# High and low parts of the values in one stationary operand, with the halves of the result added by GpSimd

## The chip, the cores and the metric

The kernel runs on one NeuronCore of a Trainium2 chip. The metric is the time of one execution on the device, in microseconds, as the median of several runs. TensorE does the matrix products and transposes and writes them to PSUM, VectorE and ScalarE read PSUM and SBUF, GpSimd works on SBUF, and the SyncE queue issues nearly all the transfers. The engines run each their own list of instructions in order and wait for each other on semaphores.

## The reference

One layer of a decoder on 1024 tokens of width 1024, in float32: sliding-window attention (16 query heads, 4 key/value heads of width 64, blocks of 128 queries that see their own block and the one before), a squared-ReLU MLP and a gated embedding. The part that matters here is the attention:

```python
q = rmsnorm(q, gq)
k = rmsnorm(k, gk)
kb, vb = band(k), band(v)          # the block before and the block itself: 256 keys
scores = einsum('bnqkgd,bnskd->bnkgqs', qb, kb) * HD ** -0.5
scores = scores - slopes[:, :, None, None] * dist
scores = where(mask, scores, -inf)
m = maximum(scores.max(axis=-1), sink)
e = exp(scores - m[..., None])
probs = e / (e.sum(axis=-1) + exp(sink - m))[..., None]
o = einsum('bnkgqs,bnskd->bnqkgd', probs, vb)
return o.reshape(b, s, H * HD) @ wo
```

## The kernel before

TensorE takes float32 data in a reduced form (`F32R`), so every operand is kept as two parts: a high part, rounded by a ScalarE copy, and a low part, which VectorE makes as the original minus the high part. A product is then three products, high·high, high·low and low·high (`PASSES`).

The attention stage goes over 8 blocks of 128 queries (`n`), and in each over 4 groups (`j`), one for each key/value head with its 4 query heads. Blocks 1 to 5 are one hardware loop, blocks 0, 6 and 7 are written out. The order is written by hand and is the same on all engines; in each group's turn work of several steps is interleaved:

- TensorE (`body`, L1808): the scores of group j, part of the projection of the next block (`project`; "q0" are query heads 0 to 7, "q8" heads 8 to 15, "k" keys and values), transposes of q or k, the product with the values of group j-2 (`weigh_values`), and the transposes of the probabilities of group j-1 (`turn_probs`).
- VectorE (`body`, L1326): bias and row maxima (L1298), the negated maximum (L1303), the reciprocal, the scaling of the probabilities as four instructions (L1316), the low parts of pT (L1323), and in group 1 the low part of the values (L1282), in group 3 that of kT (L1264).
- ScalarE (`body`, L919): the exponentials (L895), the copy of the result of group j-2 from PSUM to RES (`attention_out`, L913), the high parts of pT (L905), in group 1 the high part of the values (L868).
- GpSimd (`body`, L707): variance and power -0.5 for the norms (`head_norm`, `row_norm`), the sink column of the probabilities (`place_sinks`), and the move of keys and values from the slot "this block" to the slot "block before" (`shift_k`, `shift_v`, L680).

The values are kept in `vz`, with zeros between the heads. A stationary operand is 128 columns wide and holds the 64 values of one head beside 64 zeros; taken 64 columns further left, it holds the zeros first. So two products of 256 columns put the even heads of a group into the upper 64 partitions of one PSUM tile of 128x256 and the odd heads into the lower 64. With two slots of keys, three passes and two halves these are 12 matmuls for a group (L1799). One ScalarE copy takes the 128x256 result to RES and counts the semaphore `attended`. TensorE waits for it before the next product, since there is one PSUM bank for it (`pv_bank`).

In block 7 there is no next block to project. There the weights `wo` of the output projection are split instead: ScalarE makes high parts (`wo_hi_unit`, L821), VectorE (L1374) and GpSimd (L696) four low parts each, and TensorE begins with `project_out` (L1859). At the program's start GpSimd clears `vz` and `kT` (L651, L652) and makes the bias tables (L668), and the first block's key norm stands behind ten of these.

After the attention stage come the output projection, the MLP (L1936, L1976, L1997, L2017) and the gate (L2040, L2053), nearly all of it on TensorE without a gap.

## Time and profile before

| | us |
|---|---|
| median of 3 runs | 1142.11 (1141.85 to 1143.12) |
| profiled execution, its time | 1143.35 |
| profiled execution, span from first to last instruction | 1141.6 |
| attention stage, up to the last product with the values | 0 to 308 |
| one block in the loop | 32.8 |
| busy: TensorE / VectorE / ScalarE / GpSimd | 1107.6 / 765.5 / 453.7 / 252.9 |

Times of a trace are counted from the start of the span. A row of an engine gives the start, the duration, the line in the kernel, the tiles written and read, and in brackets how long the engine had been idle and for whom. Matmuls are pipelined: a single row is longer than the time from one to the next, and the chain of waits gives the latter.

### The profile page before, as it was taken

The page shows a single profiled execution, that of the slowest core. Times are in us where ns is not written, and L with a number is a line of the kernel's source. Part 1 is how long each engine was busy: PE and PEld are TensorE (multiplying, and loading weights), DVE is VectorE, ACT ScalarE, POOL GpSimd, SP SyncE. Part 2 cuts the span into 40 slices and gives each one's busy share as a digit, 9 for nine tenths or more (in the row PEclk, how much of TensorE's full clock was granted, in tenths as well). Part 3 has the DMA queues.
Part 4 walks back from the last instruction along what each step waited for, and adds up shares of the span by engine and source line. Part 5 has one row for each costly group of instructions (what it writes and reads, how often), then busy time and mean ns, then how long its engine had stood idle before and what let it go on. Part 6 is the DMA issues. An engine that isn't in the chain of part 4 may idle for free.

```text
span 1141.6 us, 15063 instructions
## 1 busy us (share of the span) xinstructions
PE 1107.6 (97%) x5418; PEld 930.1 (81%) x5418; DVE 765.5 (67%) x1129; ACT 453.7 (40%) x796; POOL 252.9 (22%) x230
## 2 busy tenths in 40 slices
PE   7899999998999996999999999999999999999998
PEld 6788888886888885888888888888888888888887
DVE  5788887888553588766766676668777774564321
ACT  5565666566432314233223323553333332243100
POOL 6532322323100185324532450000000000010000
PEclk9999999999999998999999999999999999999999
DMA  7000000013142404332533234899888882111211
GB/s 277 20 19 20 18 18 18 18 34 151 38 153 87 148 19 166 148 145 114 203 148 144 115 133 144 340 408 345 286 293 289 291 287 77 38 37 56 84 40 44
DMA packets 61801, 154.41 MB, mean 135 GB/s; under 512 B 5040, under 2 KB 6064, under 8 KB 61744
## 3 DMA queue, kind: packets, MB, share of 16 engines
q1 hardware_dynamic: 61600, 153.12, 37.4%
q8 instruction: 36, 0.59, 0.2%
q10 hardware_dynamic: 144, 0.52, 0.1%
q14 instruction: 21, 0.17, 0.0%
HBM read 119.55 MB, written 34.08 MB: 135 GB/s over the span
## 4 chain that ended last, share of the span: by engine, by line
PE 80%; DVE 10%; POOL 3%; ACT 3%; issue 3%; DMA 0%; ACTq 0%; DVEq 0%; POOLq 0%
PE pair L1997 23%; PE pair L1976 23%; PE pair L2040 8%; PE pair L1859 6%; PE pair L1731 5%; PE pair L2017 4%; ACT probs L895 2%; PE pair L1799 2%; PE pair L2053 2%; PE pair L1770 2%; DVE probs L1298 2%; DVE probs L1316 1%; PE pair L1936 1%; PE pair L1906 1%; PE pair L1782 1%
## 5 line engine op out<-in xcount | busy, mean ns | idle before, releaser
L1997 PE MATMUL pair<-uT 128*128 128x512 f32 x1176 | 266.7, 389 | 0.0
L1997 PEld LDWEIGHTS pair<-uT 128*128 128x128 f32 x1176 | 220.7, 188 | 45.8
L1126 ACT ACTIVATE uT<-wo_raw 128x1024 fp32r<-128x1024 f32 x63 | 63.9, 1053 | 105.0 <-PE pair L1997 89.4
L638 POOL TENSOR_SCALAR row_var<-row_ssq 128x1 f32<-128x1 f32 x24 | 4.6, 192 | 437.0 <-ACT hn L1023 430.3
L1572 DVE TENSOR_TENSOR uT<-wo_raw,uT 128x1024 fp32r<-128x1024 f32 x63 | 74.8, 1221 | 39.5 <-ACT uT L1126 39.5
L1731 PE MATMUL pair<-WA,xT 128*128 128x512 f32 x384 | 96.4, 401 | 1.4 <-DVE kn L1255 1.0
L1859 PE MATMUL pair<-WA,oT 128*128 128x512 f32 x384 | 91.6, 396 | 2.3 <-DVE WA L1374 1.7
L1859 PEld LDWEIGHTS pair<-WA,oT 128*128 128x128 f32 x384 | 72.4, 191 | 17.6 <-issue 1.9
L1731 PEld LDWEIGHTS pair<-WA,xT 128*128 128x128 f32 x384 | 70.7, 191 | 17.4 <-issue 2.9
L895 ACT ACTIVATE probs<-probs,nmax 128x257 f32<-128x257 f32 x128 | 63.7, 500 | 52.3 <-DVE nmax L1303 52.1
L1976 PE MATMUL pair<-WA,WB 128*128 128x512 f32 x312 | 74.4, 396 | 3.6 <-ACT xr L1101 3.6
L1976 PEld LDWEIGHTS pair<-WA,WB 128*128 128x128 f32 x312 | 59.6, 191 | 16.6 <-issue 4.0
L1976 PE MATMUL pair<-uT,WB 128*128 128x512 f32 x264 | 61.6, 389 | 0.0
L1976 PEld LDWEIGHTS pair<-uT,WB 128*128 128x128 f32 x264 | 49.5, 188 | 10.3
L1799 PE MATMUL pair<-pT,vz 128*128 128x256 f32 x384 | 52.5, 286 | 0.7 <-DVE pT L1323 0.7
L1799 PEld LDWEIGHTS pair<-pT,vz 128*128 128x128 f32 x384 | 48.9, 190 | 3.4 <-DVE pT L1323 2.2
L775 POOL TENSOR_TENSOR hn<-RES 128x1024 f32<-128x1024 f32 x7 | 22.3, 3187 | 120.4 <-DVE RES L1558 120.4
L1679 DVE TENSOR_TENSOR act_buf<-pair,act_buf 128x512 f32<-128x512 f32 x16 | 11.0, 690 | 55.3 <-PE pair L2053 55.3
L1298 DVE CUSTOM_DVE_ANT_0 probs<-pair,bias 128x256 f32<-128x256 f32 x128 | 46.3, 418 | 0.2 <-PE pair L1770 0.2
L1731 PE MATMUL pair<-WB,xT 128*128 128x512 f32 x192 | 45.3, 392 | 0.7 <-DVE xT L1230 0.7
L1638 DVE TENSOR_TENSOR RES<-RES,pair 128x512 f32<-128x512 f32 x48 | 30.8, 681 | 22.2 <-PE pair L1997 22.2
L2017 PE MATMUL pair<-WA 128*128 128x512 f32 x192 | 45.4, 393 | 0.0
(182 smaller groups left out, 2074.7 us busy)
## 6 DMA issues: line engine op xcount, KB each, us to landing
wo_raw<-in_m_w SPq DMA_DIRECT2D x53, 512.0 KB, 6.5
wo_raw<-hid_kept SPq DMA_DIRECT2D x36, 512.0 KB, 4.6
hid_kept<-RES SPq DMA_DIRECT2D x28, 512.0 KB, 2.6
emb<-in_m_w SPq DMA_DIRECT2D x20, 512.0 KB, 6.5
RES<-in_m_w SPq DMA_DIRECT2D x8, 1024.0 KB, 6.7
RES<-in_a_wqkv SPq DMA_DIRECT2D x12, 512.0 KB, 8.8
uT_f<-in_m_w SPq DMA_DIRECT2D x6, 1024.0 KB, 6.7
act_buf<-hid_kept SPq DMA_DIRECT2D x11, 512.0 KB, 4.6
```

The lines of the kernel that those rows point to most:

```text
L895: ex = nc.scalar.activation(row, row, ACT.Exp, bias=nmax[:, i, r:r + 1], accum_out=denom[:, i, r:r + 1])
L1126: nc.scalar.activation(operand(t, which, HI), unit(t, which), ACT.Copy).then_inc(op_hi, 1)
L1298: nc.vector.tensor_tensor_reduce(probs[:, i, r, 0:2 * P], score_bank[r // 2][:, (r % 2) * 2 * P:(r % 2 + 1) * 2 * P], bias[:, G * j + r, : ...
L1572: nc.vector.tensor_tensor(operand(t, which, LO), unit(t, which), operand(t, which, HI).bitcast(F32), ALU.subtract).then_inc(op_ready, 1)
L1638: nc.vector.tensor_tensor(RES[:, b, cols], RES[:, b, cols], bank[:], op).then_inc(posted, 1)
L1731: mm = nc.tensor.matmul(proj_bank[X][:], xT[:, s, kt, :], w[:, m, kt, at:at + BANK], start=(kt == 0 and i == 0), stop=(kt == KT - 1 and i ...
L1799: mm = nc.tensor.matmul(pv_bank[:, 0:2 * P], vz[:, kt, s, at:at + 2 * HD], pT[:, m, kt, odd * 2 * P:(odd + 1) * 2 * P], start=(done == 0), ...
L1859: mm = nc.tensor.matmul(ps[2 * odd + c][:], oT[:, hf, s, k % 4 * P:(k % 4 + 1) * P], wo_s[:, m, k, c * BANK:(c + 1) * BANK], start=(k == 0 ...
L1976: mm = nc.tensor.matmul(chain[:, m, :], a_slot[q % 4][:, s, k, m * P:(m + 1) * P], right(i)(r)[:, k, :], start=(opens and k == 0 and n == ...
L1997: mm = nc.tensor.matmul(ps[4 * (j % 2) + m][:], operand(t, 0, s)[:, k, m * P:(m + 1) * P], operand(t, 1, r)[:, k, :], start=(g == 0 and k ...
L2017: mm = nc.tensor.matmul(ps[4 + a % 4][:], hid[:, s, k, b * P:(b + 1) * P], w2_s[:, r, k, c * BANK:(c + 1) * BANK], start=(k == 0 and q == ...
L2040: mm = nc.tensor.matmul(ps[4 + s % 2][:], uT[:, u, kt, b * P:(b + 1) * P], w[:, m, kt, :], start=(kt == 0 and q == 0), stop=(kt == KT - 1 ...
```

## The change

`vz` loses its zeros: for each slot and head it now holds the 64 columns of the high part and beside them the 64 columns of the low part. One stationary operand of 128 columns is thus both parts of a head. A group takes 4 matmuls of 512 columns (two slots of keys times high and low part of pT) instead of 12 of 256; low·low is computed too. The upper 64 partitions of the PSUM bank hold the products with the high part of the values for all four heads, the lower 64 those with the low part.

ScalarE takes them out with four copies of 64x256: two go to RES, two to a new buffer `low_out` (two slots), moved across the partition halves where needed. It counts a new semaphore, `pv_copied`, for which TensorE now waits. GpSimd adds `low_out` to RES (`add_lows`) and counts `attended`; ScalarE waits for it before it writes a slot of `low_out` again. The copy of `vz` in `shift_v` has 512 columns instead of 1152, the clearing 1024 instead of 2304.

```diff
-        vz = sb("vz", [P, 2, 2, (2 * KV + 1) * HD], F32R, in_a)
+        vz = sb("vz", [P, 2, KV, 2, HD], F32R, in_a)
+        low_out = sb("low_out", [P, 2, 2 * P], F32, in_a)
...
+            def add_lows(n, j):
+
+                stand(pool, pv_copied, 4 * n + (j + 1))
+                dst = RES[:].rearrange("p b n -> p (b n)")[:, bass.ds(n * D + j * 2 * P, 2 * P)]
+                pool.tensor_tensor(dst, dst, low_out[:, j % 2, :], ALU.add).then_inc(attended, 1)
+
             def body(n, x_too=True, last=False):
                 head_norm("q8", n)
                 place_sinks(n, 1)
+                add_lows(n - 1, 2)
                 place_sinks(n, 2)
                 if last:
                     wo_lo_unit(WO_POOL[0])
+                add_lows(n - 1, 3)
                 shift_v(n)
                 if last:
                     wo_lo_unit(WO_POOL[1])
...
                 place_sinks(n, 3)
-                if not last:
+                if last:
+                    wo_lo_unit(WO_POOL[2])
+                else:
                     head_norm("k", n + 1)
+                add_lows(n, 0)
+                if last:
+                    wo_lo_unit(WO_POOL[3])
+                else:
                     shift_k(n + 1)
                     place_sinks(n + 1, 0)
+                add_lows(n, 1)
...
+            add_lows(0, 0)
             place_sinks(1, 0)
+            add_lows(0, 1)
...
-            for k in WO_POOL[2:]:
-                wo_lo_unit(k)
+            add_lows(NB - 1, 2)
+            add_lows(NB - 1, 3)
...
                 act.wait_ge(w_split, U_W1)
                 act.wait_ge(pv_done, t + 1)
+
+                wait(act, attended, t - 1)
+
+
                 dst = RES[:].rearrange("p b n -> p (b n)")[:, bass.ds(n * D + j * 2 * P, 2 * P)]
-                nc.scalar.activation(dst, pv_bank[:, 0:2 * P], ACT.Copy).then_inc(attended, 1)
+                nc.scalar.activation(dst[0:HD, :], pv_bank[0:HD, 0:2 * P], ACT.Copy)
+                nc.scalar.activation(low_out[HD:P, j % 2, :], pv_bank[HD:P, 2 * P:4 * P], ACT.Copy)
+                nc.scalar.activation(low_out[0:HD, j % 2, :], pv_bank[HD:P, 0:2 * P], ACT.Copy)
+                nc.scalar.activation(dst[HD:P, :], pv_bank[0:HD, 2 * P:4 * P], ACT.Copy).then_inc(pv_copied, 1)
...
-                wait(pe, attended, t)
+                wait(pe, pv_copied, t)
                 done = 0
                 for kt in range(2):
-                    for s, m in PASSES:
-                        for odd in range(2):
-                            at = 2 * HD * j + (0 if odd else HD)
-                            mm = nc.tensor.matmul(pv_bank[:, 0:2 * P], vz[:, kt, s, at:at + 2 * HD],
-                                                  pT[:, m, kt, odd * 2 * P:(odd + 1) * 2 * P],
-                                                  start=(done == 0), stop=(done == 11))
-                            done += 1
+                    for m in (HI, LO):
+                        mm = nc.tensor.matmul(pv_bank[:], vz[:, kt, j, :, :].rearrange("p s d -> p (s d)"),
+                                              pT[:, m, kt, :], start=(done == 0), stop=(done == 3))
+                        done += 1
                 mm.then_inc(pv_done, 1)
```

GpSimd's list in the loop, from the norm of q8 to that of q0 (`probs<-sink` is `place_sinks`, `vz<-vz` is `shift_v`), before:

```order
L647 TENSOR_TENSOR q_rstd<-q_var,half 128x8 [waits q8_var_ready]
L403 REGISTER_ALU
L704 TENSOR_SCALAR probs<-sink 128x4 [waits exps_done]
L403 REGISTER_ALU
L704 TENSOR_SCALAR probs<-sink 128x4 [waits exps_done]
L680 TENSOR_SCALAR vz<-vz 128x1152 [waits pv_done]
L403 REGISTER_ALU
L645 TENSOR_SCALAR q_var<-q_ssq 128x8 [waits q0_summed]
```

The same place after:

```order
L706 TENSOR_SCALAR probs<-sink 128x4 [waits exps_done]
L405 ISA
L713 ISA [waits pv_copied]
L713 TENSOR_TENSOR RES<-RES,low_out 128x256
L405 REGISTER_ALU
L706 TENSOR_SCALAR probs<-sink 128x4 [waits exps_done]
L405 REGISTER_ALU
L713 ISA [waits pv_copied]
L713 TENSOR_TENSOR RES<-RES,low_out 128x256
L682 TENSOR_SCALAR vz<-vz 128x512 [waits pv_done]
L405 REGISTER_ALU
L647 TENSOR_SCALAR q_var<-q_ssq 128x8 [waits q0_summed]
```

The copy of the values stood behind a wait for TensorE alone; it now stands behind an add that waits for ScalarE's copies.

GpSimd's list in the last block, from its first sink column on (`WA<-wo_raw,WA` is a low part of wo), before:

```order
L704 TENSOR_SCALAR probs<-sink 128x4 [waits exps_done] x2
L696 TENSOR_TENSOR WA<-wo_raw,WA 128x1024 [waits wo_hi]
L680 TENSOR_SCALAR vz<-vz 128x1152 [waits pv_done]
L696 TENSOR_TENSOR WA<-wo_raw,WA 128x1024 [waits wo_hi]
L704 TENSOR_SCALAR probs<-sink 128x4 [waits exps_done]
L696 TENSOR_TENSOR WA<-wo_raw,WA 128x1024 [waits wo_hi] x2
```

The same place after:

```order
L706 TENSOR_SCALAR probs<-sink 128x4 [waits exps_done]
L713 TENSOR_TENSOR RES<-RES,low_out 128x256 [waits pv_copied]
L706 TENSOR_SCALAR probs<-sink 128x4 [waits exps_done]
L698 TENSOR_TENSOR WA<-wo_raw,WA 128x1024 [waits wo_hi]
L713 TENSOR_TENSOR RES<-RES,low_out 128x256 [waits pv_copied]
L682 TENSOR_SCALAR vz<-vz 128x512 [waits pv_done]
L698 TENSOR_TENSOR WA<-wo_raw,WA 128x1024 [waits wo_hi]
L706 TENSOR_SCALAR probs<-sink 128x4 [waits exps_done]
L698 TENSOR_TENSOR WA<-wo_raw,WA 128x1024 [waits wo_hi]
L713 TENSOR_TENSOR RES<-RES,low_out 128x256 [waits pv_copied]
L698 TENSOR_TENSOR WA<-wo_raw,WA 128x1024 [waits wo_hi]
L713 TENSOR_TENSOR RES<-RES,low_out 128x256 [waits pv_copied] x3
```

An add stands ahead of three of the four low parts of wo, and one ahead of the copy of the values. VectorE's list is the same in both kernels.

## Rows read from the trace of the kernel before

**Rows 1.** The page, busy time by engine: us (share of the span).
```profile
PE 1107.6 (97%) x5418; PEld 930.1 (81%) x5418; DVE 765.5 (67%) x1129; ACT 453.7 (40%) x796; POOL 252.9 (22%) x230
```
**Rows 2.** Stretches: length, busy us of PE, PEld, DVE, ACT, POOL, clock, DMA share, GB/s.
```profile
139.21:171.99 32.78, 32.17 (x207) 28.62 (x206) 26.95 (x80) 20.92 (x59) 8.73 (x14) 1.00 0.05 16
171.99:204.76 32.77, 32.20 (x206) 28.60 (x206) 26.94 (x80) 20.95 (x59) 8.73 (x14) 1.00 0.05 16
...
270.00:308.00 38.00, 33.01 (x188) 27.76 (x187) 29.29 (x69) 22.62 (x56) 12.72 (x7) 0.96 0.06 19
```
**Rows 3.** Waits from 139.21 to 204.76 (two blocks): us in total, times, longest.
```profile
PE pair L1770 <- DVE kT L1264: 1.2, 2, 0.6
```
**Rows 4.** The chain of waits, whole span, longest pieces: start us, us, what.
```profile
134.81 1.22 PE pair L1770 x8
136.90 1.44 PE pair L1799 x12
...
140.17 3.43 PE pair L1731 x15
...
167.59 1.22 PE pair L1770 x8
```
**Rows 5.** The chain of waits from 138 to 173, every piece.
```profile
143.60 0.45 PE pair L1755 x4
...
149.00 0.93 DVE probs L1316 x4
...
151.33 0.42 DVE vz L1282
...
166.60 0.76 DVE kT L1264
```
**Rows 6.** Instructions in order of time, group 1 of a block: start us, us, engine.
```profile
147.74 1.17 POOL L680 TENSOR_SCALAR vz<-vz 128x1152 fp32r<-128x1152 f32 x1 [7.30 <-PE pair L1799]
...
148.18 0.38 ACT L913 ACTIVATE RES<-pair 128x256 f32 x1
...
148.44 1.09 ACT L905 ACTIVATE pT<-pair 128x512 fp32r<-128x512 f32 x2
148.92 1.17 DVE L1316 TENSOR_SCALAR probs<-probs,rden 128x256 f32<-128x256 f32 x4
...
149.40 0.44 ACT L868 ACTIVATE vz<-vnext 128x256 fp32r<-128x256 f32 x1
```
**Rows 7.** GpSimd's lines: ns of one, min/median/max; the 128x2048 row: busy us, ns.
```profile
L696 POOL TENSOR_TENSOR WA<-wo_raw,WA x4: 2362/2776/3363, 271.1 to 293.5; 128x1024 fp32r<-128x1024 f32 x4
...
L761 POOL TENSOR_TENSOR WA_f<-uT 128x2048 f32<-128x2048 f32 x1 | 4.6, 4606 | 5.4 <-DVE uT L1438 5.4
...
L680 POOL TENSOR_SCALAR vz<-vz x7: 1161/1164/1172, 82.2 to 278.4; 128x1152 fp32r<-128x1152 f32 x7
...
L651 POOL MEMSET vz<- x1: 2019/2019/2019, 8.4 to 8.4; 128x2304 f32 x1
```
**Rows 8.** Instructions in order of time, group 2 of the same block.
```profile
158.30 1.06 POOL L680 TENSOR_SCALAR kT<-kT 128x1024 fp32r<-128x1024 f32 x1 [0.66 <-PE pair L1770]
...
158.49 1.80 DVE L1316 TENSOR_SCALAR probs<-probs,rden 128x256 f32<-128x256 f32 x4
```
**Rows 9.** Instructions in order of time in the last block, GpSimd, VectorE and TensorE.
```profile
271.08 3.36 POOL L696 TENSOR_TENSOR WA<-wo_raw,WA 128x1024 fp32r<-128x1024 f32 x1
...
272.12 3.27 DVE L1316 TENSOR_SCALAR probs<-probs,rden 128x256 f32<-128x256 f32 x4
...
293.50 2.77 POOL L696 TENSOR_TENSOR WA<-wo_raw,WA 128x1024 fp32r<-128x1024 f32 x1 [5.34 <-ACT WA L821]
...
295.43 0.86 DVE L1303 SCALAR_TENSOR_TENSOR nmax<-rmax,nsink 128x4 f32<-128x4 f32 x1
...
301.04 1.70 PE L1799 MATMUL pair<-pT,vz 128*128 128x256 f32 x12
```
**Rows 10.** VectorE at the start, in order of time.
```profile
25.28 0.69 DVE L1255 TENSOR_TENSOR kn<-pair,k_rstd 128x512 f32<-128x512 f32 x1 [2.35 <-POOL k_rstd L647]
```

11 lines of the change are left out of this document (4 added, 7 removed).

## The prediction, made before the changed kernel was run

> **What bounds the kernel now.** I read the shares of busy time first. TensorE is busy 97% of the span [rows 1], so fewer matmul columns look like time saved. That share is a mean over stages, so next come the stretches of the attention stage, where the change lies. In its blocks TensorE is busy 32.2 of 32.8 us, VectorE 27, ScalarE 21, GpSimd 9 [rows 2]. Then the waits: two blocks hold two waits of TensorE of 0.6 us, both for VectorE's low part of kT [rows 3]. A wait that comes once in each block at the same place means that the loop has a chain longer than TensorE's work, and the chain of waits shows its course.
>
> Take a block from its first scores matmul (134.81) to the next block's (167.59): 32.78 us [rows 4]. The chain runs on TensorE up to the end of the q8 transposes (143.60 + 0.45 = 144.05) [rows 4, 5]. From there to 167.59 it is not on TensorE at all: q8 is copied, then exponentials of group 1 on ScalarE, probabilities scaled (149.00), pT low parts, values' low part (151.33), bias and exponentials of group 2, key norm on GpSimd, scaling, group 3, and last kT's low part (166.60 + 0.76) [rows 5]. So the loop is 9.24 us of TensorE and 23.54 us of ScalarE, VectorE and GpSimd. Of the four P·V products of a block exactly one (136.90, 1.44 us) lies on the chain; the other three run while the second leg is under way.
>
> **TensorE.** 12 matmuls of 256 columns take 1.44 us [rows 4]. The new ones have 512 columns, like the projection's: 15 in 3.43 us, 0.229 us each [rows 4]. Four take 0.91 us, so 0.53 us is saved per group, 2.1 us per block. On the chain lies one group: **-0.5 us per block**. The rest becomes idle time of TensorE (about 3 us per block instead of 0.6).
>
> The Trainium skill (TensorE: Matmul & The Clock Gate, Back-to-back issue gap) gives about 131 ns for a 512-column matmul in a stream of load and matmul pairs. The projection's row shows 229 ns in such a stream, so the measurement decides. By the page the product would take 0.52 us, and the time would be 6 × 0.4 = 2.4 us below my forecast.
>
> **ScalarE.** One copy of 256 columns becomes four of 256 columns on 64 partitions. The copy at 148.18 is followed at 148.44 by the next instruction [rows 6]: 0.26 us each. A copy's price follows its columns, and each half still has 256, so I take no discount for fewer partitions: three more are +0.78 us per group, 3.1 us per block on an engine with 12 us free. They stand behind the exponentials and ahead of the pT high parts. In group 1 the pT high parts then start at 149.2 instead of 148.44; VectorE wants the first at 150.1, with the scaling done, so this alone costs nothing. At the turn of the block pT's high parts move by the same 0.8 and VectorE's path to group 1's maximum by some tenths; that path runs beside TensorE's leg and has slack, since the copies of q8 follow on the leg alone: 0 to +0.1.
>
> **GpSimd.** Its add of two 128x256 SBUF tiles has no row. 128x1024 took at least 2.36 us and 128x2048 4.60 us [rows 7], 2.19 ns per column and 0.12 fixed: 0.68 us. The copy of vz shrinks from 1152 columns (1.16 us) to 512; kT's 1024 took 1.06 us [rows 7, 8], so 0.82 ns per column and 0.22 fixed: 0.64 us.
>
> Now group 1, where it matters. Before, the vz copy starts at once when the P·V product of the last group is done (147.74) and ends at 148.91 [rows 6]. In the new order it stands behind the add, and the add waits for ScalarE's fourth copy: 148.18 + 3 × 0.26 + 0.38 = 149.35, so it can start near 149.5. VectorE is at that moment in the middle of its four scalings (148.92 to 150.09) [rows 6]. What happens when these meet is shown ten us later: the scaling of group 2 takes 1.80 us where kT's copy runs beside it [rows 8], against 1.17 [rows 6]: VectorE stood still for 0.65 us until GpSimd was done. Three outcomes:
> - GpSimd gets in between two scalings: VectorE loses about 0.6 us, on the chain.
> - VectorE keeps going: the add starts at 150.1, the vz copy ends at 151.5, ScalarE's high part of the values (0.44 us [rows 6]) at 152.0, and VectorE's low part, which was at 151.33, comes 0.7 us late.
> - No conflict: the vz copy still ends at 150.95 and the high part at 151.45, 0.15 us late.
> I take 0.7, which two of the three give; the ends are 0.15 and 1.2 (both GpSimd operations get in).
>
> In group 2 the add stands ahead of kT's copy. It ends near 158.45, so the copy starts 0.25 us later than its 158.30 and keeps VectorE's scaling (158.49) that much longer: **+0.25** (0 to 0.3). The other two adds of a block meet waits that are long.
>
> **A block** is then -0.5 + 0.7 + 0.25 + 0.05 = +0.5 us (-0.4 to +1.0). Six periods of the loop (from block 1's first scores to block 7's) make **+3.0** (-2.4 to +6).
>
> **The last block** has no projections, so TensorE already waits: 33.0 of 38 us busy [rows 2]. GpSimd does four low parts of wo there, and two collisions show their price: the scaling at 272.12 took 3.27 us beside one, the tiny maximum at 295.43 took 0.86 us beside another [rows 9]. Step by step, against the times of before: (1) In group 0 the first low part of wo comes behind an add, starts some 1.9 us later (after 0.78 of copies, 0.68 of add, a sink column) and falls into the scaling as before: +1. (2) In group 1 the vz copy, until now at 278.4 [rows 7], waits for ScalarE's copies behind the exponentials, four or five us later, then takes 0.68 + 0.64; the values' low part comes +1.1. (3) ScalarE's next two high parts of wo stand behind its high part of the values, so VectorE's low part of wo, in front of group 2's bias, comes +1.7. (4) GpSimd's third wo part ends later by that and by an add and holds group 2's maximum: +2.3. (5) Group 3 repeats it with three copies more (0.78) on ScalarE less what idle time absorbs: +2.7 at the last exponentials. From there TensorE is the bound (its product at 301.04, and everything after), and it has two products less to do: 1.70 - 0.91 and 0.53, so 2.7 - 1.3 = **+1.4** (-1 to +2.5).
>
> **The start.** The memset of vz shrinks from 2304 to 1024 columns: 2.02 us for 2304 [rows 7] makes 0.9, **-1.1**. It is on the chain: VectorE sat idle 2.35 us for GpSimd's key norm [rows 10], so all of it comes through. The ten bias rows in between collide with VectorE less when earlier: -1.3 (-0.5 to -2). In block 0 one product is on the chain: 0 to -0.5, I take -0.3.
>
> **Sum:** -1.3 - 0.3 + 3.0 + 1.4 = +2.8 us. Behind the attention stage nothing changes. The profiled execution has a span of 1141.6 us and took 1143.35; added to its time this makes 1146.2, added to the median of the runs, 1142.11, about **1145**. I predict the median.
>
> **Rivals.**
> - *TensorE is the bound after all* (97% [rows 1]; against it the waits [rows 3] and a second leg without TensorE [rows 5]). Then all 32 groups give 0.53: -17, and with the start 1124 to 1128. This is the change's face value. 7%.
> - *The adds slip past VectorE*: 0.15 in group 1, nothing in group 2, -0.3 per block, and the last block +0.7: 1139 to 1141. For it: a tiny GpSimd operation beside the scaling cost nothing. 20%.
> - *Both GpSimd operations get in*, the add and the vz copy, each between two scalings: 1.2 in group 1, +1.0 per block: 1148. It decides if the add arrives while two scalings are left. The Trainium skill (SBUF — State Buffer, Who interferes with whom) says that GpSimd shares a port pair with VectorE that whoever starts first holds for the whole instruction; by that rule the 1.80 us is explained, and this rival follows where GpSimd arrives early. 13%.
> - *TensorE's clock falls in the loop.* It stands at 1.00 with 0.6 us of idle time and at 0.96 in the stretch with 5 us [rows 2]. Each block will have about 3 us, in three gaps near 1 us. If half of the 9.2 us leg went at half speed once per block, say +1.5 us each, it is 1154. 6%.
> - *512-column matmuls stream faster* than the projection's: 1142.7. 4%.
>
> **Numbers.** The forecast itself has 40%, with 1142.5 to 1148; 10% I leave to what I don't see. A measurement of this kernel can tell about 0.2%, 2.3 us. Faster than that (under 1139.8) are the first rival, a third of the second, and a little of the unseen: 0.17. Slower (over 1144.4) are three quarters of the forecast, the third and fourth rivals and some of the unseen: 0.52. Within: 0.31. The range goes from 1138 to 1151, which leaves out the first and fourth rivals.
>
> **What the changed profile would show.** TensorE's busy time falls by about 17 us to some 1090, yet the span doesn't. The block's period is 33.3 us. TensorE waits over 1 us for kT once per block, and near 1 us each before the q0 transposes and the q8 projection. The add takes 0.68 us, and group 1's scaling over 1.6 us or values' low part waits for ScalarE. GpSimd's key norm ends 1.1 us earlier. A period under 32.5 us would refute my reading of the meeting in group 1; one near 30.8 the chain itself. In the last block the last exponentials should come 2 to 3 us later, counted from its first scores; if not, that term is wrong.

## The result, and the profile after

The changed kernel takes 1149.24 us (median of 6 runs, 1148.02 to 1151.71), the kernel before 1142.01 us beside it (6 runs, 1140.94 to 1143.12). The ratio is 1.0067 (95% interval 1.0053 to 1.0081): slower by 0.7%, some 7.2 us. The forecast was slower, at 1145, some 3 us: the sign was right and the size too small by more than half. The measured time lies inside the range that I gave (1138 to 1151), and outside the 1142.5 to 1148 that I gave the forecast itself.

The profiled execution has a span of 1149.9 us, 8.3 more than the 1141.6 of before. Its page, busy time by engine, answers to [rows 1]:

```profile
PE 1099.7 (96%) x5162; PEld 909.8 (79%) x5162; DVE 768.5 (67%) x1129; ACT 491.8 (43%) x892; POOL 270.3 (24%) x262
```

TensorE has 256 matmuls and 8 us less, and the span is longer: what it saved came back as idle time and more. ScalarE has 38 us more for 96 more instructions, GpSimd 17 us more for 32 adds. The next lines are groups of instructions (busy us, mean ns of one, idle time of the engine just before them and what ended it): the add, VectorE's low parts of pT, and the same low parts in the kernel before (L1323). The last line is one block of the loop in the form of [rows 2]:

```profile
L713 POOL TENSOR_TENSOR RES<-RES,low_out 128x256 f32 (+1 forms) x32 | 23.8, 743 | 134.6 <-ACT RES L936 134.5
L1344 DVE TENSOR_TENSOR pT<-pair,pT 128x512 fp32r<-128x512 f32 x64 | 41.2, 684 | 15.7 <-ACT pT L921 15.7
...
L1323 DVE TENSOR_TENSOR pT<-pair,pT 128x512 fp32r<-128x512 f32 x64 | 41.0, 682 | 2.5 <-ACT pT L905 2.3
...
135.36:168.93 33.57, 30.76 (x172) 25.79 (x173) 27.34 (x79) 25.75 (x71) 10.89 (x18) 1.00 0.05 16
```

A block takes 33.57 us instead of 32.77 [rows 2], at full clock, and TensorE is busy 30.8 of them instead of 32.2. The second row is the one that I had not expected: VectorE's low parts of pT wait 15.7 us in all for ScalarE's high parts (line 921), where they waited 2.3 before.

**A block cut into five legs.** The points are the end of kT's low part on VectorE and the starts of the exponentials of the four groups on ScalarE. In the changed kernel they are these (order of time; start us, us, engine), and the legs of all kernels below are read in the same way:

```profile
134.37 0.75 DVE L1287 SCALAR_TENSOR_TENSOR kT<-pair,gk_col,kT 128x512 fp32r<-128x512 f32 x1
...
139.24 0.51 ACT L911 ACTIVATE probs<-probs,nmax 128x257 f32<-128x257 f32 x1 [1.11 <-DVE nmax L1324]
...
146.30 0.51 ACT L911 ACTIVATE probs<-probs,nmax 128x257 f32<-128x257 f32 x1
...
154.63 0.51 ACT L911 ACTIVATE probs<-probs,nmax 128x257 f32<-128x257 f32 x1 [1.04 <-DVE nmax L1324]
...
164.44 0.51 ACT L911 ACTIVATE probs<-probs,nmax 128x257 f32<-128x257 f32 x1 [3.38 <-DVE nmax L1324]
...
167.94 0.75 DVE L1287 SCALAR_TENSOR_TENSOR kT<-pair,gk_col,kT 128x512 fp32r<-128x512 f32 x1
```

kT ends at 135.12, so the legs are 4.12, 7.06, 8.33, 9.81 and 4.25 us. Before they are 3.40, 7.61, 7.77, 9.74 and 4.26. The turn of the block and group 1 are what grew.

**The turn and group 1**, in order of time, ScalarE, VectorE and GpSimd together; the second half answers to [rows 6]:

```profile
141.22 0.36 ACT L933 ACTIVATE RES<-pair 64x256 f32 x1
...
141.56 1.14 DVE L1337 TENSOR_SCALAR probs<-probs,rden 128x256 f32<-128x256 f32 x4
141.60 0.38 ACT L934 ACTIVATE low_out<-pair 64x256 f32<-64x256 f32 x1
141.99 0.38 ACT L935 ACTIVATE low_out<-pair 64x256 f32<-64x256 f32 x1
142.38 0.38 ACT L936 ACTIVATE RES<-pair 64x256 f32 x1
142.78 1.09 ACT L921 ACTIVATE pT<-pair 128x512 fp32r<-128x512 f32 x2
143.03 0.73 POOL L713 TENSOR_TENSOR RES<-RES,low_out 128x256 f32 x1 [3.11 <-ACT RES L936]
143.41 1.29 DVE L1344 TENSOR_TENSOR pT<-pair,pT 128x512 fp32r<-128x512 f32 x2 [0.70 <-ACT pT L921]
...
149.65 1.14 DVE L1337 TENSOR_SCALAR probs<-probs,rden 128x256 f32<-128x256 f32 x4
...
150.70 0.73 POOL L713 TENSOR_TENSOR RES<-RES,low_out 128x256 f32 x1 [6.78 <-ACT RES L936]
151.10 1.29 DVE L1344 TENSOR_TENSOR pT<-pair,pT 128x512 fp32r<-128x512 f32 x2 [0.31 <-ACT pT L921]
151.40 0.63 POOL L682 TENSOR_SCALAR vz<-vz 128x512 fp32r<-128x512 f32 x1
...
152.12 0.42 ACT L884 ACTIVATE vz<-vnext 128x256 fp32r<-128x256 f32 x1 [0.57 <-POOL vz L682]
...
152.57 0.43 DVE L1303 TENSOR_TENSOR vz<-vnext,vz 128x256 fp32r<-128x256 f32 x1 [0.19 <-ACT vz L884]
```

The copies start 0.39 us apart (141.60, 141.99, 142.38, then 142.78), not 0.26. Four take 1.57 us. VectorE has its scaling done at 142.70 and waits 0.70 us for the first high part of pT. The same wait (0.62 us) stands in front of group 0's bias and makes the 4.12. In group 1 the scaling is undisturbed (1.14 us): the add comes only at 150.70, later than I thought, and meets nothing. What is late is pT's high part (0.31) and, behind add and vz copy, the values' high part (0.57 on ScalarE, 0.19 on VectorE).

**Group 2**, which answers to [rows 8]:

```profile
158.95 0.73 POOL L713 TENSOR_TENSOR RES<-RES,low_out 128x256 f32 x1
...
159.64 1.06 POOL L682 TENSOR_SCALAR kT<-kT 128x1024 fp32r<-128x1024 f32 x1
...
159.76 1.88 DVE L1337 TENSOR_SCALAR probs<-probs,rden 128x256 f32<-128x256 f32 x4
```

The add ends before the scaling and the copy of kT falls into it, as before: 1.88 us instead of 1.80.

**Where the 8.3 us of the profiled execution are.** kT's low part of block 1 ends at 67.95 (before 69.03): -1.1. Six periods are 201.18 (before 196.34): +4.8. From kT's low part of block 7 to the run of 72 matmuls that closes the output projection it is 269.13 to 314.72, 45.59 us (before 265.37 to 307.65, 42.28): +3.3. Behind that, 835.2 (before 833.9): +1.3. That last part runs the same instructions in both kernels, and in the profiles of the other kernels below it is 832.4 to 835.4 with no relation to what was changed, so I put it down to the execution and not to the change; no run shows what makes it. Without it, the sum is +7.0, and the medians differ by 7.2.

### The profile page after: what moved, and what is told of

Its sections match the earlier page's. It is cut to its first block, busy times and chain, and to the rows that moved or that the text cites. A ratio compares the mean times of both kernels' runs of the same rounds, so it can differ in the third digit from the quotient of the medians.

```text
span 1149.9 us, 14759 instructions
## 1 busy us (share of the span) xinstructions
PE 1099.7 (96%) x5162; PEld 909.8 (79%) x5162; DVE 768.5 (67%) x1129; ACT 491.8 (43%) x892; POOL 270.3 (24%) x262
## 4 chain that ended last, share of the span: by engine, by line
PE 68%; DVE 3%; POOL 1%; issue 0%; ACT 0%; ACTq 0%; DVEq 0%
PE pair L2015 23%; PE pair L1994 23%; PE pair L2058 8%; PE pair L1877 6%; PE pair L2035 4%; PE pair L2071 2%; PE pair L1954 1%; PE pair L1924 1%; POOL RES L794 1%; DVE WA_f L1508 1%; DVE WA_f L1504 1%; DVE WA_f L1499 0%; DVE WA L1524 0%; DVE WA_f L1512 0%; DVE RES L1491 0%
## 5 line engine op out<-in xcount | busy, mean ns | idle before, releaser
L713 POOL TENSOR_TENSOR RES<-RES,low_out 128x256 f32 (+1 forms) x32 | 23.8, 743 | 134.6 <-ACT RES L936 134.5
L1344 DVE TENSOR_TENSOR pT<-pair,pT 128x512 fp32r<-128x512 f32 x64 | 41.2, 684 | 15.7 <-ACT pT L921 15.7
L1218 ACT ACTIVATE act_buf<-pair 128x512 f32<-128x512 f32 x16 | 9.6, 598 | 89.7 <-PE pair L2058 84.0
L1791 PE MATMUL pair<-kT,qT 128*128 128x256 f32 x256 | 38.4, 292 | 8.5 <-DVE kT L1287 5.0
```

The costliest lines, as they stand in the source:

```text
L1344: nc.vector.tensor_tensor(pT[:, LO, kt, :], pT_bank[kt][:], pT[:, HI, kt, :].bitcast(F32), ALU.subtract).then_inc(pT_ready, 1)
L1791: mm = nc.tensor.matmul(dst, qT[:, G * j + r, :], kT[:, m, j, :, :].rearrange("p a n -> p (a n)"), start=(m == HI), stop=(m == LO))
```

## The experiments

Two theories stood after this comparison. **C**: ScalarE's copies are the cost, since they hold up what stands behind them. **G**: GpSimd's adds are the cost, since they fall into VectorE's work or hold up GpSimd's own copies. The table gives for each kernel the time, its ratio to the kernel before with the interval, the five legs of one block of the loop and the period (their sum), and the last block from kT's low part to the run of 72 matmuls. Where there is one run only, no interval stands.

| kernel | us | ratio | legs | period | last block |
|---|---|---|---|---|---|
| before | 1142.0 | | 3.40, 7.61, 7.77, 9.74, 4.26 | 32.78 | 42.28 |
| changed | 1149.2 | 1.0067 (1.0053 to 1.0081) | 4.12, 7.06, 8.33, 9.81, 4.25 | 33.57 | 45.59 |
| shift_first | 1148.3 | 1.0055 (1.0038 to 1.0072) | 4.12, 7.06, 8.03, 9.81, 4.26 | 33.28 | 45.02 |
| pt_first | 1158.1 | 1.0137 (1.0120 to 1.0154) | 3.89, 6.93, 9.31, 10.35, 4.26 | 34.74 | 47.40 |
| both_orders | 1148.4 | 1.0052 (1.0035 to 1.0069) | 3.89, 6.93, 8.00, 10.37, 4.25 | 33.44 | 46.67 |
| two_copies | 1145.2 | 1.0028 (1.0018 to 1.0037) | 3.39, 7.15, 8.61, 9.74, 4.26 | 33.15 | 44.03 |
| copies_alone | 1148.7 | 1.0053 (1.0038 to 1.0069) | 4.13, 7.07, 8.03, 9.30, 4.27 | 32.80 | 46.99 |
| no_add | 1144.0 | 1.0020 (1.0011 to 1.0029) | 4.12, 7.07, 8.02, 9.08, 4.26 | 32.55 | 46.97 |
| same_half | 1149.4 | one run | 4.12, 7.08, 8.35, 9.78, 4.26 | 33.59 | 45.61 |
| full_copies | 1143.5 | one run | 3.65, 6.93, 8.23, 9.73, 4.26 | 32.80 | 44.63 |
| best | 1138.7 | 0.9976 (0.9966 to 0.9987) | 3.39, 7.10, 7.77, 9.09, 4.25 | 31.60 | 46.31 |
| best2 | 1136.9 | 0.9951 (0.9937 to 0.9965) | 3.39, 7.10, 7.76, 9.09, 4.25 | 31.59 | 43.67 |
| before_order | 1142.3 | 1.0008 (0.9999 to 1.0017) | 3.39, 7.60, 7.78, 9.72, 4.26 | 32.75 | 42.54 |

### shift_first: the vz copy ahead of the add

```diff
                     wo_lo_unit(WO_POOL[0])
-                add_lows(n - 1, 3)
                 shift_v(n)
+                add_lows(n - 1, 3)
```

> The changed kernel with one thing moved on GpSimd: the copy of vz stands ahead of the add of group 3 instead of behind it. In the changed kernel a block takes 33.57 us. Theory C (ScalarE's four copies, 1.57 us to the next instruction instead of 0.26, hold the high parts of pT, and VectorE's low parts wait for them): only the wait for the high part of the values goes, 0.2 us per block, period 33.35, time about 1148. Theory G (GpSimd's order and its collisions with VectorE make the loss): 0.5 to 0.7 us per block come back, period 32.9 to 33.1, time 1145.

Measured: 1148.3 us, period 33.28. One leg changed, group 1, by 0.30: the values' high part no longer waits for GpSimd. Here is group 1 in order of time; ScalarE goes from pT's high parts straight to the values:

```profile
149.69 1.09 ACT L921 ACTIVATE pT<-pair 128x512 fp32r<-128x512 f32 x2
149.92 0.73 POOL L713 TENSOR_TENSOR RES<-RES,low_out 128x256 f32 x1 [2.26 <-ACT RES L936]
150.31 1.29 DVE L1344 TENSOR_TENSOR pT<-pair,pT 128x512 fp32r<-128x512 f32 x2 [0.32 <-ACT pT L921]
150.66 0.42 ACT L884 ACTIVATE vz<-vnext 128x256 fp32r<-128x256 f32 x1
```

So of the 0.56 us that group 1 lost, 0.30 is the vz copy behind the add and 0.26 is pT's high part behind the copies (the 0.32 of idle time is still there).

### pt_first: pT's high parts ahead of the copies

```diff
                         k_hi_part(n + 1)
-                    if not (first and j < 2):
-                        attention_out(*before(n, j, 2))
                     if not (first and j < 1):
                         pT_hi_part(t - 1)
+                    if not (first and j < 2):
+                        attention_out(*before(n, j, 2))
```

> The changed kernel with one thing moved on ScalarE: in each group the two high parts of pT stand ahead of the four copies of the result. Theory C: VectorE waits no longer for the high parts of pT (0.7 us at the turn of the block, 0.3 in group 1); but GpSimd's add, and with it the copy of vz behind it, come 1.1 us later, so the low part of the values comes 0.8 us later. Period 33.2 to 33.6, time 1147 to 1149. Theory G: nothing is won at the turn and more is lost in group 1: period 34.2, time 1153.

Measured: 1158.1 us, a period of 34.74. Both theories were too low. The wait for pT's high part is gone, as C wanted, but everything that hangs on the last copy comes a good microsecond later. The first three rows are group 1 and the last three group 2 of the same block:

```profile
188.31 0.74 POOL L713 TENSOR_TENSOR RES<-RES,low_out 128x256 f32 x1 [6.63 <-ACT RES L936]
189.02 0.63 POOL L682 TENSOR_SCALAR vz<-vz 128x512 fp32r<-128x512 f32 x1
...
190.19 0.42 DVE L1303 TENSOR_TENSOR vz<-vnext,vz 128x256 fp32r<-128x256 f32 x1 [1.45 <-ACT vz L884]
...
197.38 2.41 DVE L1337 TENSOR_SCALAR probs<-probs,rden 128x256 f32<-128x256 f32 x4
197.53 0.79 POOL L713 TENSOR_TENSOR RES<-RES,low_out 128x256 f32 x1 [0.99 <-ACT RES L936]
198.30 1.09 POOL L682 TENSOR_SCALAR kT<-kT 128x1024 fp32r<-128x1024 f32 x1
```

In group 1 the vz copy, still behind the add, now makes VectorE wait 1.45 us. In group 2 the add comes while the scaling runs, and the kT copy right behind it: both get in between two scalings, and four scalings take 2.41 us, against 1.14 undisturbed. That is the third rival of the prediction, in group 2 instead of group 1.

### both_orders: the two together

The edits are those of the two runs above.

> Both moves at once: high parts of pT ahead of the four copies on ScalarE, copy of vz ahead of the add on GpSimd. All instructions are the same as in the changed kernel. Theory C: the wait at the turn (0.7) and in group 1 (0.5, less 0.15 for the values' high part behind the copies) go: period 32.5, below the 32.77 of the kernel before, time 1141 to 1142. Theory G: only the vz part goes, period 33.0, time 1145 to 1146.

Measured: 1148.4 us, neither the 1141 to 1142 of C nor the 1145 to 1146 of G. Group 1 is back at 8.00, yet group 2 stays at 10.37 with the same scaling of 2.41 us (191.48) and the same two operations of GpSimd inside it. C alone is refuted by this; so is G alone by shift_first, which gave back 0.3 us of a block and not 0.5 to 0.7. When ScalarE hands over its last copy decides into which VectorE instruction GpSimd falls.

### two_copies: two copies of 128 rows instead of four of 64

The halves that should cross don't, so the sums are not the attention's.

```diff
-                nc.scalar.activation(dst[0:HD, :], pv_bank[0:HD, 0:2 * P], ACT.Copy)
-                nc.scalar.activation(low_out[HD:P, j % 2, :], pv_bank[HD:P, 2 * P:4 * P], ACT.Copy)
-                nc.scalar.activation(low_out[0:HD, j % 2, :], pv_bank[HD:P, 0:2 * P], ACT.Copy)
-                nc.scalar.activation(dst[HD:P, :], pv_bank[0:HD, 2 * P:4 * P], ACT.Copy).then_inc(pv_copied, 1)
+                nc.scalar.activation(low_out[:, j % 2, :], pv_bank[:, 2 * P:4 * P], ACT.Copy)
+                nc.scalar.activation(dst, pv_bank[:, 0:2 * P], ACT.Copy).then_inc(pv_copied, 1)
```

> The changed kernel with two copies of 128x256 instead of four of 64x256 (the halves aren't moved across the partitions, so the sums are not those of the reference). GpSimd's work is the same. Theory C: ScalarE needs 0.52 instead of 1.57 us there, the waits of VectorE go: period 32.5, time 1141 to 1142. Theory G: GpSimd's add now comes 1 us earlier and falls into VectorE's scaling in group 1, which my forecast priced at 0.6 us: period 33.2 to 33.4, time 1147 to 1148.

Measured: 1145.2 us, between the two. With 0.5 us of copies the turn is as before (3.39) and the product's gain shows (3.39 + 7.15 is 10.54, before 11.01). But group 1 now has the collision that I had forecast for the changed kernel:

```profile
181.20 2.00 DVE L1335 TENSOR_SCALAR probs<-probs,rden 128x256 f32<-128x256 f32 x4
181.38 0.76 POOL L713 TENSOR_TENSOR RES<-RES,low_out 128x256 f32 x1 [6.66 <-ACT RES L934]
182.11 0.67 POOL L682 TENSOR_SCALAR vz<-vz 128x512 fp32r<-128x512 f32 x1
```

The add arrives 0.18 us into the scaling and both operations get in: 2.00 us and a group 1 of 8.61, 0.84 more than before. The slower copies of the changed kernel had kept the add out of it.

### copies_alone: the kernel before with four copies

```diff
-                nc.scalar.activation(dst, pv_bank[:, 0:2 * P], ACT.Copy).then_inc(attended, 1)
+                nc.scalar.activation(dst[0:HD, :], pv_bank[0:HD, 0:2 * P], ACT.Copy)
+                if spare is not None:
+                    nc.scalar.activation(spare[HD:P, :], pv_bank[HD:P, 0:2 * P], ACT.Copy)
+                    nc.scalar.activation(spare[0:HD, :], pv_bank[HD:P, 0:2 * P], ACT.Copy)
+                nc.scalar.activation(dst[HD:P, :], pv_bank[HD:P, 0:2 * P], ACT.Copy).then_inc(attended, 1)
```

> The kernel before, with one part of the change alone: ScalarE brings each attention output out in four copies of 64 rows instead of one of 128 (two go to a place that the next block writes over, so the output stays that of the kernel before). No adds, the old products, the old vz. Theory C (the change's loss comes from ScalarE's time: 0.39 us per copy, so 1.57 us instead of 0.26 per group, paid at the turn of the block and in front of group 1's pT high parts): turn +0.7, group 1 +0.3 to +0.5, so a period of 33.7 to 34.0 instead of 32.77, the last block +2 to +3, no gain at the start: 1149 to 1152. Theory G (the loss comes from what GpSimd does beside VectorE's scalings): a period of 32.8 to 33.0, 1142 to 1143.5.

Measured: 1148.7 us, just under C's 1149 to 1152, but not where C said: the period is 32.80, which was G's. The turn did grow by 0.73 and group 1 by 0.26, and yet the period stays: the turn's delay is almost hidden by TensorE's leg, which is as long as before (4.13 + 7.07 is 11.20, before 11.01), and group 2 fell from 9.74 to 9.30, since VectorE comes to its scaling later and the kT copy is almost done by then (kT copy at 157.99, scaling at 158.63, 1.34 us). The cost is in the last block: 46.99 instead of 42.28. VectorE waits 7.2 us there for the high parts of pT, which stand behind the copies, and 2.3 in the kernel before. These 4.7 us and 1.5 behind the attention stage (835.4 instead of 833.9) make the 6.1 by which the profiled spans differ; the medians differ by 6.7.

### no_add: the changed kernel without the adds

The low halves are left out of the sum. ScalarE's last copy gives the signal that the add gave.

```diff
             def add_lows(n, j):
-                stand(pool, pv_copied, 4 * n + (j + 1))
-                dst = RES[:].rearrange("p b n -> p (b n)")[:, bass.ds(n * D + j * 2 * P, 2 * P)]
-                pool.tensor_tensor(dst, dst, low_out[:, j % 2, :], ALU.add).then_inc(attended, 1)
+                return
```

> The changed kernel without GpSimd's adds: the four copies stay, the low halves are left out of the sum, so the output lacks the low part of the values. Theory C: the period stays near 33.3 to 33.5 (0.1 to 0.2 less than 33.57, since the vz copy no longer stands behind an add), the last block gives back some 0.5 to 1: 1146.5 to 1148. Theory G: without adds nothing falls into a scaling that did not before, so the period is 32.3 to 32.5 and the time 1138 to 1140.

Measured: 1144.0 us, a period of 32.55. The period is 1.02 us shorter than the changed kernel's, near G's 32.3 to 32.5 and far from C's; the time is between the two, since the last block didn't gain. Of the 1.02 us, 0.31 are in group 1 (the vz copy is no longer behind an add, the same as in shift_first) and 0.73 are in group 2. The second is the surprise. Rows of group 2 in order of time:

```profile
155.47 1.05 POOL L681 TENSOR_SCALAR kT<-kT 128x1024 fp32r<-128x1024 f32 x1
...
156.33 1.14 DVE L1333 TENSOR_SCALAR probs<-probs,rden 128x256 f32<-128x256 f32 x4
```

Here the kT copy starts 0.86 us ahead of the scaling, where in the kernel before it was 0.19 [rows 8]. It is in its last 0.2 us when the scaling begins, no delay shows, and the collision of [rows 8], which cost the kernel before 0.65 us in each block, is gone. The change had freed it; the add in front of the kT copy took it back. The turn (4.12) didn't gain, and the last block (46.97) is as long as in copies_alone: they are the copies'.

### same_half and full_copies: why a copy takes 0.39 us

Two kernels with four copies each. In the first each of the four reads and writes the same half of the partitions. In the second all four have 128 rows (three go to spare slots; the add reads one slot, so ScalarE waits for the add of the group just before and not of the one before that). In neither are the sums the attention's.

```diff
-                nc.scalar.activation(low_out[0:HD, j % 2, :], pv_bank[HD:P, 0:2 * P], ACT.Copy)
-                nc.scalar.activation(dst[HD:P, :], pv_bank[0:HD, 2 * P:4 * P], ACT.Copy).then_inc(pv_copied, 1)
+                nc.scalar.activation(low_out[0:HD, j % 2, :], pv_bank[0:HD, 0:2 * P], ACT.Copy)
+                nc.scalar.activation(dst[HD:P, :], pv_bank[HD:P, 2 * P:4 * P], ACT.Copy).then_inc(pv_copied, 1)
```

> The changed kernel with the four copies of 64 rows each reading and writing the same half of the partitions; the halves that should cross do not, so the sums are not the attention's. If the 0.39 us between two copies are a matter of 64 rows (or of two copies that read different halves of one bank), they stay 0.39 apart and the time is that of the changed kernel, 1148 to 1150. If it is the crossing from one half of the partitions to the other, the copies stand 0.26 apart, a group takes 1.05 us instead of 1.57, and the time is 1145 to 1147.

```diff
+                nc.scalar.activation(low_out[:, 0, :], pv_bank[:, 2 * P:4 * P], ACT.Copy)
+                nc.scalar.activation(low_out[:, 1, :], pv_bank[:, 2 * P:4 * P], ACT.Copy)
+                nc.scalar.activation(low_out[:, 2, :], pv_bank[:, 2 * P:4 * P], ACT.Copy)
+                nc.scalar.activation(dst, pv_bank[:, 0:2 * P], ACT.Copy).then_inc(pv_copied, 1)
```

> The changed kernel with four copies of 128 rows instead of four of 64 (three of them of the low columns into spare slots; the sums are not the attention's). If 64 rows are what makes the copies 0.39 us apart, these stand 0.26 apart, four take 1.05 us, and the turn's wait of VectorE shrinks from 0.70 to about 0.2; what GpSimd's add falls into decides the rest: 1144 to 1149. If four copies from one bank are slow whatever their rows, they stay 0.39 apart and the block keeps 4.12 us from kT's low part to the first exponentials.

ScalarE in order of time, first same_half, then full_copies:

```profile
140.09 0.36 ACT L933 ACTIVATE RES<-pair 64x256 f32 x1
140.47 0.38 ACT L934 ACTIVATE low_out<-pair 64x256 f32<-64x256 f32 x1
140.86 0.38 ACT L935 ACTIVATE low_out<-pair 64x256 f32<-64x256 f32 x1
```

```profile
138.01 0.36 ACT L933 ACTIVATE low_out<-pair 128x256 f32<-128x256 f32 x1
138.27 0.37 ACT L934 ACTIVATE low_out<-pair 128x256 f32<-128x256 f32 x1
138.54 0.37 ACT L935 ACTIVATE low_out<-pair 128x256 f32<-128x256 f32 x1
138.80 0.38 ACT L936 ACTIVATE RES<-pair 128x256 f32 x1
139.07 1.09 ACT L921 ACTIVATE pT<-pair 128x512 fp32r<-128x512 f32 x2
```

One instruction is as long in both (0.36 to 0.38). With 128 rows the next starts 0.26 us later and overlaps it; with 64 rows the next waits for the end, 0.39. The crossing is ruled out, since same_half has none and its time, 1149.4, is the changed kernel's. That it is the 64 rows as such is not shown apart: every 64-row instruction in these traces is followed by one that writes from another first partition (the other half, or all 128 rows), and no run has two copies of the same half in a row. A copy of 64 rows behind an instruction of 128 rows does overlap it (in the changed kernel kT's high part starts at 166.54 and takes 0.69 us, the first copy starts at 167.13).

With the price that I had assumed, the block takes 32.80 us instead of 33.57, so the wrong price is 0.77 of the period. That is a net figure: in full_copies the add comes at 147.03 and falls into group 1's scaling, which takes 1.62 us instead of 1.14, a loss that the slow copies had kept away. The time, 1143.5 in one run, is 0.5 below the range expected. The Trainium skill (ScalarE: Activation LUTs, What ACT_TABLE_LOAD costs) says that instructions of ScalarE one behind the other overlap by about 93 ns; the 128-row copies agree (0.37 long, 0.26 apart), the 64-row copies don't.

### best: both orders put right

On ScalarE pT's and the values' high parts go ahead of the copies, and at the turn the copies wait until the squares for q8's norm are out. On GpSimd the adds go where VectorE doesn't scale. The cuts leave out GpSimd's own list for the last block, where the adds and the copy of the values move against the parts of wo as well.

```diff
                         part_squares("q8", n)
+                        if not first:
+                            attention_out(*before(n, 0, 3))
...
-                    if not (first and j < 2):
-                        attention_out(*before(n, j, 2))
                     if not (first and j < 1):
                         pT_hi_part(t - 1)
                     if j == 1:
                         v_hi_part(n)
...
+                    if not (first and j < 2) and (j < 3 or last):
+                        attention_out(*before(n, j, 2))
```

```diff
                 head_norm("q8", n)
+                add_lows(n - 1, 0)
+                add_lows(n - 1, 1)
                 place_sinks(n, 1)
-                add_lows(n - 1, 2)
                 place_sinks(n, 2)
...
-                add_lows(n - 1, 3)
+                add_lows(n - 1, 2)
                 shift_v(n)
...
                     row_norm(x_squared, x_var, x_rstd, n + 2)
+                add_lows(n - 1, 3)
                 place_sinks(n, 3)
...
-                add_lows(n, 0)
...
-                add_lows(n, 1)
```

> The changed kernel with both of its costs moved, nothing left out. On ScalarE the pT high parts and the values' high part go ahead of the four copies, and at the turn the copies wait until the squares of q8. On GpSimd the adds stand where VectorE does not scale: two behind the q8 norm, one behind the third sink column ahead of the vz copy, one behind the row norm; none is in front of the vz copy of its own group or of kT's. If the loss is the sum of both (C and G together), the period falls to 32.0 to 32.3 (32.77 of before, less 0.5 on TensorE, and no new wait), the start keeps its 1.2 us and the last block costs 1 to 2: 1136 to 1139. Theory C alone would have the same. Theory G alone, or a GpSimd operation that still falls into the scaling of group 2 (it cost 0.5 in the run with both orders): 32.6 to 32.8, 1140 to 1142. If the deferred copies hold the next P.V product (the bank is free only then), the period is above 33 and the time above 1144.

Measured: 1138.7 us, faster than the kernel before by 0.24%. The period is 31.60, 1.17 less than before and below the 32.0 to 32.3 expected. Each leg now says what it holds: the turn and the leg behind it take 10.49 together (11.01 before, the product's 0.52), group 1 takes 7.77 as before, and group 2 takes 9.09, since the kT copy starts 0.86 us ahead of the scaling, as in no_add. In the last block it loses 4.0 us where I expected 1 to 2, more than the changed kernel.

### best2: the last block

```diff
                 place_sinks(n, 1)
-                place_sinks(n, 2)
                 if last:
                     wo_lo_unit(WO_POOL[0])
+                place_sinks(n, 2)
...
                     place_sinks(n, 3)
-                    add_lows(n - 1, 3)
                     wo_lo_unit(WO_POOL[2])
+                    add_lows(n - 1, 3)
...
+                    if last and j == 2:
+                        attention_out(n, 0)
                     exps(n, j)
...
-                    if not (first and j < 2) and (j < 3 or last):
+                    if not (first and j < 2) and (j < 3 or last) and not (last and j == 2):
                         attention_out(*before(n, j, 2))
```

> The reordered changed kernel with its last block mended: GpSimd's first and third low parts of wo start one step earlier (ahead of a sink column, ahead of an add), and ScalarE's four copies of group (7,0) go into its idle time ahead of group 2's exponentials. In the reordered kernel the scaling of group 0 took 3.26 us beside the first of these parts and a maximum 2.32 us beside the third, and a P.V product waited 3.85 us for the copies. If the last block's cost is a matter of these three places, it shrinks by 2 to 4 us: 1135 to 1137. If the parts of wo only fall into other VectorE instructions, the time stays at 1138 to 1139. Loop and start as in the reordered kernel.

Measured: 1136.9 us, faster than before by 0.49%; the last block is 43.67, shorter by 2.6. GpSimd's first part of wo, 1.2 us earlier, now keeps VectorE's part of wo (2.35 us instead of 1.22) and no longer the scaling (1.13 instead of 3.26), and the maximum beside the third part takes 0.85 instead of 2.32. The product that had waited 3.85 us for the copies waits 1.81 for pT. The profiled executions of best and best2 have the same span (1135.4 and 1135.5), because the part behind the attention stage, where they don't differ, took 2.7 us longer in the second; the gain of 1.8 us is that of the medians. Here is the first place:

```profile
262.11 2.38 POOL L698 TENSOR_TENSOR WA<-wo_raw,WA 128x1024 fp32r<-128x1024 f32 x1
...
263.21 2.35 DVE L1399 TENSOR_TENSOR WA<-wo_raw,WA 128x1024 fp32r<-128x1024 f32 x1
265.49 1.13 DVE L1341 TENSOR_SCALAR probs<-probs,rden 128x256 f32<-128x256 f32 x4
```

### before_order: ScalarE's new order in the kernel before

The edit is the first one of best, on the kernel before.

> The kernel before with ScalarE's new order alone (pT high parts and values' high part ahead of its single copy, the turn's copy behind the squares of q8; nothing on GpSimd moves). Theory C+G: with one copy of 0.26 us there was nothing at this place to gain, so the loop stays at 32.7 to 32.8 and the time within 0.2% of before; the gain of the reordered changed kernel is then the product's. If instead the order alone is what gained, the period falls to 32.2 or less and the time below 1139.

Measured: ratio 1.0008 (0.9999 to 1.0017), and no leg moved by more than 0.02. So the order alone gives nothing with one copy of 0.26 us; it is needed only to carry the change. The 1.17 us per block of best are the product (0.52) and the kT copy that comes clear of the scaling (0.65).

## Why the prediction was right in sign and short in size

The mechanism of the forecast, a product that pays little and two other engines that lose more, was right. The price of ScalarE's copies was wrong, the terms for group 1 and group 2 were too high, those for the start and the last block too low, and part of the errors cancelled; that the time stayed inside the range is owed to its width too. The third rival's 1148 is nearer to the measured time than my 1145, but what it said, both GpSimd operations inside group 1's scaling, did not happen.

**The bound** was read rightly: fewer matmul columns gave nothing by themselves. TensorE lost 256 matmuls, the span grew, and TensorE waits 1.2 us for kT and 1.0 for the key norm in a block, as forecast (0.4 ahead of the q0 transposes, where I had said 1). Its busy time fell by 8 us, not by the 17 forecast: by 1.4 in a block and not by 2.1; the runs don't show why. The first rival (-17 us) never came near. Nor did the fourth in the loop, where the granted clock stayed at 1.00. Four matmuls of 512 columns on the chain gave 0.52 us, as the projection's row said: leg one and two of best are 10.49 against 11.01. By the 131 ns of the Trainium skill (TensorE: Matmul & The Clock Gate, Back-to-back issue gap) it would have been 0.9 (an estimate, 1.44 less 4 × 0.131); this case doesn't bear that figure out.

**ScalarE** is the step that failed. "I take no discount for fewer partitions" missed the opposite case: here a copy of half the partitions cost more, since the next could not overlap it. The copy of 0.26 us was really 0.39. The trace of before had a row that warned of it, and I priced from the wrong neighbour. ScalarE's line 885 of the kernel before brings q's halves out with 64 rows, and line 877 brings kT out with 128 rows, as many columns and a factor too:

```profile
144.16 1.40 ACT L885 ACTIVATE qT<-pair,gq_s 64x512 fp32r<-64x512 f32 x2 [2.87 <-PE pair L1755]
...
263.22 0.69 ACT L877 ACTIVATE kT<-pair,gk_col 128x512 fp32r<-128x512 f32 x1
```

One with a factor takes 0.69 us (0.68 with 64 rows), and two of 64 rows take 1.40, twice as long: they don't overlap. Pairs of 128 rows without a factor (0.60 us each) take 1.06 to 1.09 and do. "I take 0 to +0.1" at the turn of the block became 0.69 (11.18 instead of 10.49): it ate the product's 0.52 and more. My argument there, that the path beside TensorE's leg has slack, was sound for 0.3 us and not for 0.7.

**Group 1.** Forecast +0.7, measured +0.56, by another course, so the near hit is luck. I had listed a collision and a late vz copy; it was the late vz copy (0.30, shown by shift_first) and pT's high part behind the copies (0.26), which I had ruled out with "this alone costs nothing". The forecast of a scaling over 1.6 us was wrong (1.14), that values' low part waits for ScalarE right (0.19).

**Group 2.** Forecast +0.25, measured +0.07, and the zero was in the wrong place: I took the kT copy's collision as given and asked how much longer the add would make it. Without the add it would have vanished (9.09 instead of 9.74). What the add costs here is 0.7, hidden in a difference of 0.07.

**A block**: +0.80 instead of +0.5, six of them +4.8 instead of +3.0.

**The last block**: +3.3 instead of +1.4. The last exponentials start 34.20 us behind kT's low part instead of 30.95, so +3.25 where +2.7 was forecast. The steps were of the right kind, not of the right size. The first scaling even gained (1.62 instead of 3.27), and two others lost. VectorE in order of time in the last block of the changed kernel:

```profile
279.30 2.19 DVE L1395 TENSOR_TENSOR WA<-wo_raw,WA 128x1024 fp32r<-128x1024 f32 x1
...
288.70 2.06 DVE L1303 TENSOR_TENSOR vz<-vnext,vz 128x256 fp32r<-128x256 f32 x1
...
307.51 1.29 DVE L1344 TENSOR_TENSOR pT<-pair,pT 128x512 fp32r<-128x512 f32 x2 [0.70 <-ACT pT L921]
```

The low part of the values took 2.06 us instead of 0.42 beside a part of wo. And "from there TensorE is the bound" failed: behind the last exponentials VectorE waits 0.70 us (the row at 307.51) and 2.94 us for pT's high part, and TensorE's product at 308.85 waits 1.15 for pT, so the two products' gain of 1.3 did not come: from the last exponentials to the run of 72 matmuls it is 11.4 us, before 11.3. copies_alone and no_add have this cost and more (46.99 and 46.97), both without the adds, one with the old product and one with the new, so it is the copies'. How it splits between copies, wo parts and collisions was not measured apart; full_copies keeps 2.4 of it with the cheaper copies.

TensorE's clock fell here, which I had looked for in the loop alone. The last block's row for the changed kernel, in the form of [rows 2]:

```profile
269.23:307.81 38.58, 31.50 (x144) 24.24 (x144) 29.60 (x75) 29.46 (x71) 17.53 (x15) 0.87 0.06 23
```

The granted clock is 0.87, against 0.96 in the kernel before; it averages 0.62 from 276 to 285 and 0.52 from 291 to 294, nearly all of it at the lower of the clock's two levels, after waits of TensorE of 1.7 us (until 276.79) and 2.5 us (until 290.53) for the low parts of wo. It is not what makes the last block long: over the last block as counted in the table, copies_alone has 46.99 us at a clock of 0.96, as high as before, and best2 43.67 at 0.88.

**The start**: -1.1 instead of -1.6. The smaller memset takes 0.95 us instead of 2.02, as worked out; the 0.3 us of the product in block 0 and 0.2 of the bias rows did not show.

So the terms were -1.1, +4.8 and +3.3 where I had -1.6, +3.0 and +1.4. The price of a 64-row copy is 0.77 of a period, measured by full_copies, and 4.6 us in six: more than the 4.2 that are missing. So the errors partly cancelled: with copies at my price a block came out at +0.02, not at my +0.5.

## What to carry to other kernels

A shorter product pays only on the chain; on any other engine that its result must pass, each added instruction has to be priced from a row with the same number of partitions and the same halves, not only as many columns, and then placed: behind what the next stage waits for, and where no VectorE instruction runs that GpSimd would stop. A collision that stands in the profile is not a constant: ask of each shift whether it removes one, and of each added GpSimd operation which VectorE instruction it will find running. Here the same change, at the same arithmetic, was worth +1.4%, +0.7% or -0.5% by order alone (pt_first, the changed kernel, best2).

## What the runs showed of the hardware

- A ScalarE copy of one half of the partitions doesn't overlap a follower that writes from another first partition: 0.39 us from start to start for 256 columns, against 0.26 for 128 rows behind each other (same_half, full_copies), and two of 512 columns with a factor took 1.40 us at 0.68 each. Whether two copies of the same half would overlap no run shows. Four copies of 64 rows take 1.57 us where one of 128 rows took 0.26.
- Which VectorE instructions GpSimd stops: the scalings (1.14 us alone, 2.00 and 2.41 with two GpSimd operations beside them) and the low parts of the values and of wo (0.42 and 1.2 alone, 2.06 and 2.19), but not the low part of pT, which takes 1.29 us beside the add at 143.03 and 1.28 without one. By the Trainium skill (SBUF — State Buffer, Who interferes with whom) a VectorE instruction with two inputs in SBUF contends with GpSimd's reads, and one with at most one, outside the fast modes, doesn't. The trace agrees for values and wo (two in SBUF) and for pT (one in PSUM). The scaling reads one tensor from SBUF and was stopped, so by that rule it must run in a fast mode, a condition that the prediction left out. A scaling alone takes 0.33 to 0.35 us, the low part of the values, with as many columns, 0.42; that fits, but no run here shows the mode.
- VectorE lets GpSimd in between two instructions of a series: of four scalings of pt_first, begun first at 197.38, the second took 0.83 us beside the add and the third 1.14 beside the kT copy, the fourth again 0.33, and the four took 1.27 us longer (2.41). In no_add a kT copy in its last 0.2 us and a sink column of 0.26 us beside the scaling cost nothing.
